# One encoder layer on one core: x handed over in feature order too, and the GLA value projection computed first from x times the norm's vector

## The chip, the cores and the metric

The kernel runs on one core of one Trainium2 chip. The metric is the device time of one execution in microseconds (us). A core has TensorE (matmuls, into eight PSUM banks), VectorE, ScalarE, GpSimd and SyncE; the DMA engines move data between HBM and the core's memory, SBUF. Every engine works through its own instructions in order and waits on semaphores for the others.

## What is computed

A token stream x of 512 tokens by 1024 features goes through one encoder layer: a mixer of neighbourhood attention (NA) and gated linear attention (GLA), then a mixture of 32 experts, then a last norm. The change touches only the first norm and the projections from it, and leaves what is computed as it is. Cut to that:

```python
def rmsnorm(x, g):
    xf = x.astype(jnp.float32)
    y = xf * lax.rsqrt(jnp.mean(xf * xf, axis=-1, keepdims=True) + RMS_EPS)
    return (y * g.astype(jnp.float32)).astype(x.dtype)

def hybrid_mixer(h, w_in, ...):                  # h = rmsnorm(x, norm_mix_g)
    proj = h @ w_in                              # (512 x 1024) @ (1024 x 3104)
    na_q, na_k, na_v, g_q, g_k, g_v, g_r, g_lf, g_lb = jnp.split(proj, cuts, axis=-1)
    ...
```

The parts g_q and g_k (256 columns each) are the GLA queries and keys, g_v (512) its values, g_r (512) its output gate, g_lf and g_lb (16 each) the low-rank inputs of its decay gates. The decay is log_sigmoid(low rank @ w_g2 + b) / 16, summed up within chunks of 64 tokens. All is float32.

The norm's factor of a token, 1/sqrt(mean square + eps), is one number per token, and the norm's vector is one number per feature. So h @ w is (x times the vector) @ w, with each token's result multiplied by its factor.

## The kernel before, in words

The kernel is one function, `mixer_and_moe`, with one instruction stream per engine; the order on each engine is written out by hand, and semaphores tie the streams together. SBUF is one arena in which `at(KiB, ...)` gives a buffer a fixed place, so buffers that lie over each other order the work too.

The start, up to what the change touches:

- **SyncE** (from L347) issues all loads: four token tiles of x (L350, 512 KB each, rows of 4 KB), the constants `small` with the identity matrix (L352, 224 KB), the norm's vector `gmix`, the gate bias, the low-rank weights `w_lr` (L355, 128 KB), `w_g2`, then the weights of the first two groups of 512 columns (L358, 2 MB each): GLA queries and keys, GLA values. Then come the position bias, its mask and late constants. Further groups are loaded into `w_buf` when the group that last used the buffer is done (L369).
- **ScalarE** squares each token tile with a running sum and takes the root (L903, L905); **VectorE** makes mean and reciprocal (L1141, L1143) and scales the tile by the factor into `xs` (L1145).
- **TensorE** transposes each tile in eight pieces (L471); the eight banks then hold x in feature order, eight chunks of 128 features by 512 tokens. VectorE and ScalarE empty them in turn, times the norm's vector, into `hT` (L1150, L899).
- **TensorE** then computes the low-rank product (L509, eight matmuls of 32 columns in four column groups), one unit of queries, the four gate matmuls (L517), three more units of queries and keys, four units of values, four of the output gate. A *unit* is eight matmuls that add up the eight chunks in one bank (`unit`, L487). Units use banks 0 and 1 in turn, the value units banks 2 to 5. ScalarE empties them (`gla_q_evict`, `gv_evict`, L954, L955).
- The gates: ScalarE adds the bias (L926), takes absolute value, exponential and logarithm (L931, L933, L935); VectorE subtracts (L1154), scans by chunk (L1159) and takes differences; ScalarE takes exponentials (L938, L939, L943, L948), VectorE and GpSimd make from them and the queries and keys `q_rel`, `q_exp`, `k_rel` (L1577) and `k_dec` (L1579).
- **GpSimd** builds the 24 bias tables of NA first (L1567), as soon as the mask has landed.

After that TensorE transposes `k_dec` (L532), computes the GLA scores, the NA queries, keys and values with GLA states between them, both attentions, the output projection and the routing. The expert weights (6 MB each expert) are loaded by SyncE upon events of TensorE, the first ones when unit 25 is done (L382); the expert stage begins near 300 us and goes on to 765 us.

Of the kernel before, what the change touches and what calls it, by code (L numbers as in the profile page):

```python
# [60 lines left out]
GV_UNITS = range(5, 9)  # L61
GR_FIRST = range(9, 9 + UNIT_BANKS)
# [25 lines left out]
def mixer_and_moe(nc, x, rpb, w_in, w_g2, b_g, gla_g, g_mix, w_out, g_ffn_T, w_r, b_r, w_gate, w_up, w_down, g_fin,  # L88
                  c_small, c_mask, c_scan, c_tok, out, limit=SLOTS):
    with ExitStack() as ctx:  # L90
# [28 lines left out]
        r_exp = at(78, TT, 512)  # L119
# [4 lines left out]
        xs = at(102, TT, D)  # L124
# [24 lines left out]
        junk = at(179, TT, D)  # L149
# [124 lines left out]
        win_in = [sem(f"win_in{g}") for g in range(7)]  # L274
        og_done, og_added, wog_in, router_ready = sem("og_done"), sem("og_added"), sem("wog_in"), sem("router_ready")
        sumsq_done, ms_done, root_done, rstd_done = sem("sumsq_done"), sem("ms_done"), sem("root_done"), sem("rstd_done")
        xs_done, small_in = sem("xs_done"), sem("small_in")
        xT_done, hT_act, hT_vec = sem("xT_done"), sem("hT_act"), sem("hT_vec")
        unit_done, unit_evicted = sem("unit_done"), sem("unit_evicted")
        gates_done, z_done, abs_done, expa_done = sem("gates_done"), sem("z_done"), sem("abs_done"), sem("expa_done")  # L280
        softp_done, g_done, scan_done, d1_done = sem("softp_done"), sem("g_done"), sem("scan_done"), sem("d1_done")
# [61 lines left out]
        groups = [("lr", None, IN_LR), ("gqk", 0, IN_GQK), ("gv", 1, IN_GV), ("gr", 0, IN_GR),  # L343
# [4 lines left out]
        def _(sp):  # L348
            for t in range(TT):
                sp.dma_start(x1[:, t], x_d[t]).then_inc(x_in_sb[t], 16)  # L350
                if t == 0:
                    sp.dma_start(small[:, 0:448], c_small).then_inc(small_in, 16)  # L352
            sp.dma_start(gmix, g_mix).then_inc(consts_in, 16)
            sp.dma_start(bg, b_g).then_inc(consts_in, 16)
            sp.dma_start(w_lr, win_d[:, :, IN_LR:IN_LR + 2 * RANK]).then_inc(win_in[0], 16)  # L355
            sp.dma_start(gE[:, 0], w_g2).then_inc(consts_in, 16)
            for g in (1, 2):
                sp.dma_start(w_buf[groups[g][1]], win_d[:, :, groups[g][2]:groups[g][2] + 512]).then_inc(win_in[g], 16)  # L358
# [15 lines left out]
            sp.dma_start(w_og[1], wout_d[:, 3 * KC // 4:]).then_inc(wog_in, 16)  # L374
            sp.dma_start(wr_sb, w_r).then_inc(g2_in, 16)
# [90 lines left out]
        def _(pe):  # L466
            pe.wait_ge(small_in, 16)
            for t in range(TT):
                pe.wait_ge(xs_done, t + 1)
                for k in range(KC):  # L470
                    m = pe.transpose(pbank[k][:, t * P:(t + 1) * P], xs[:, t, k * P:(k + 1) * P], ident)  # L471
                    if t == TT - 1:
                        m.then_inc(xT_done, 1)
# [1203 lines left out]
```

## Time and profile before

| | before |
|---|---|
| median of 3 runs | 790.31 us (789.97 to 791.11) |
| profiled execution, its own time | 789.99 us |
| its span | 788.2 us |
| TensorE busy | 735.7 us (93%) |
| VectorE / ScalarE / GpSimd busy | 226.4 / 146.5 / 85.5 us |
| DMA | 234.76 MB, mean 298 GB/s |
| first 20 us: TensorE busy, DMA | 11.1 us, 326 GB/s |

The span is the profiled part of the execution, from its first to its last instruction. Rows of the trace give engines as PE (TensorE matmuls), PEld (its weight loads), DVE (VectorE), ACT (ScalarE), POOL (GpSimd) and SP (SyncE). A float32 matmul of 128x512 leaves two records. PEclk is the granted clock of TensorE as a share of full speed, 2.4 GHz. "L487" is line 487 of the kernel; what stands behind "<-" in square brackets is what ended the engine's idle time.

### The profile page before, as it was taken

What the parts mean: (1) busy time and instruction counts of PE and PEld (TensorE: products, weight loads), DVE (VectorE), ACT (ScalarE), POOL (GpSimd) and SP (SyncE); (2) the same over time, 40 slices, a digit from 0 to 9 for tenths busy, and PEclk for the clock granted to TensorE, in tenths of its full rate; (3) what the DMA queues carried; (4) which work ended last, traced back from release to release, by engine and by line L of the source; (5) the groups of instructions that cost most, each with busy time, mean ns of one, the idle gap of its engine ahead of it and who ended that gap; (6) DMA issues with size and microseconds to landing.
All of it is one profiled execution on the core that took longest, in us unless ns stands there. A gap on an engine that the chain in (4) does not pass through costs nothing.

```text
span 788.2 us, 13656 instructions
## 1 busy us (share of the span) xinstructions
PE 735.7 (93%) x6148; PEld 371.3 (47%) x6148; DVE 226.4 (29%) x455; ACT 146.5 (19%) x319; POOL 85.5 (11%) x81
## 2 busy tenths in 40 slices
PE   5999999999999999999999999999999899988950
PEld 3444454464455466555454455545445355433510
DVE  3008782005566257211111111111111111111126
ACT  5252330024255443000000000000000000000004
POOL 0542340000000121000000000000000000000002
PEclk9999999999999999999999999999999999999995
DMA  9430230401450548999999999999999999999964
GB/s 325 120 106 20 87 108 1 160 4 59 184 243 2 229 197 352 377 422 428 424 422 428 423 426 421 425 425 423 425 426 423 424 421 421 420 420 420 410 264 198
DMA packets 36828, 234.76 MB, mean 298 GB/s; under 512 B 5778, under 2 KB 7186, under 8 KB 18976
## 3 DMA queue, kind: packets, MB, share of 16 engines
q1 hardware_dynamic: 34208, 229.66, 71.5%
q0 software_dynamic: 2560, 4.20, 1.4%
q8 instruction: 50, 0.82, 0.4%
q14 instruction: 10, 0.08, 0.0%
HBM read 227.55 MB, written 10.49 MB: 302 GB/s over the span
## 4 chain that ended last, share of the span: by engine, by line
PE 74%; DMA 19%; SPq 2%; ACT 2%; DVE 1%; issue 1%; DVEq 0%; POOLq 0%
PE bank L487 21%; PE bank L792 18%; DMA arena<-in_w_up 17%; PE bank L815 10%; PE bank L772 8%; PE bank L655 4%; PE bank L699 3%; SPq L419 2%; PE bank L616 1%; PE bank L688 1%; PE bank L673 1%; PE bank L794 1%; PE bank L795 1%; PE bank L804 1%; DMA arena<-in_x 1%; PE bank L718 1%
## 5 line engine op out<-in xcount | busy, mean ns | idle before, releaser
L792 PE MATMUL bank<-arena 128*64 128x512 f32 x928 | 207.0, 597 | 11.4 <-DMA arena<-in_w_up 10.6
L487 PE MATMUL bank<-arena 128*128 128x512 f32 x384 | 167.0, 594 | 0.0
L792 PEld LDWEIGHTS bank<-arena 128*64 128x64 f32 x928 | 68.5, 138 | 144.9 <-issue 135.1
L815 PE MATMUL bank<-arena 128*64 128x512 f32 x512 | 116.9, 598 | 0.5 <-ACT arena L1100 0.5
L487 PEld LDWEIGHTS bank<-arena 128*128 128x128 f32 x384 | 72.3, 190 | 89.8 <-issue 88.6
L772 PEld LDWEIGHTS bank<-arena 128*128 128x128 bf16 x3072 | 96.2, 98 | 23.9 <-issue 23.4
L772 PE MATMUL bank<-arena 128*128 128x64 bf16 x3072 | 100.6, 193 | 0.0
L1095 ACT ACTIVATE arena<-bank,arena 128x256 f32<-128x256 f32 x32 | 15.2, 474 | 359.8 <-PE bank L792 316.4
L1602 POOL DMA_INDIRECT y_tok<-arena x32 | 31.2, 976 | 432.4 <-DVE arena L1473 404.4
L1466 DVE SCALAR_TENSOR_TENSOR arena<-bank,arena 128x256 f32<-128x256 f32 x32 | 15.5, 483 | 214.2 <-ACT arena L1095 214.2
L815 PEld LDWEIGHTS bank<-arena 128*64 128x64 f32 x512 | 33.9, 136 | 57.1 <-issue 54.5
L1137 DVE TENSOR_TENSOR arena<-bank,arena 128x256 f32<-128x256 f32 (+1 forms) x64 | 34.2, 555 | 84.4 <-PE bank L772 67.6
L1137 DVE TENSOR_TENSOR arena<-arena 128x512 f32<-128x512 f32 (+9 forms) x75 | 47.1, 648 | 11.3 <-ACT arena L948 4.0
L1473 DVE COPY arena<-bank 128x512 f32<-128x512 f32 x32 | 22.1, 692 | 94.7 <-PE bank L815 94.7
L655 PE MATMUL bank<-arena 128*128 128x512 f32 x64 | 31.5, 617 | 0.0
L699 PE MATMUL bank<-arena 128*128 128x512 f32 x64 | 28.4, 594 | 0.0
L1595 POOL TENSOR_TENSOR arena<-arena 128x512 bf16<-128x512 f32 x8 | 9.3, 1157 | 174.2 <-ACT arena L1051 174.2
L1100 ACT COPY arena<-bank 128x256 f32<-128x256 f32 x32 | 12.0, 374 | 64.1 <-PE bank L804 64.1
L1567 POOL TENSOR_TENSOR arena<-arena 128x256 f32<-128x256 f32 x24 | 19.4, 845 | 27.8 <-DMA arena<-in_c_mask 27.8
L699 PEld LDWEIGHTS bank<-arena 128*128 128x128 f32 x64 | 11.8, 190 | 13.4 <-issue 13.4
L794 PE MATMUL bank<-arena 128*64 128x256 f32 x96 | 15.6, 381 | 2.1 <-DMA arena<-in_w_up 2.1
L1137 DVE TENSOR_TENSOR arena<-arena,bank 128x512 f32<-128x512 f32 (+1 forms) x17 | 11.1, 654 | 20.3 <-PE bank L699 12.6
(161 smaller groups left out, 466.8 us busy)
## 6 DMA issues: line engine op xcount, KB each, us to landing
arena<-in_w_down SPq DMA_DIRECT2D x31, 2048.0 KB, 30.8
arena<-in_w_gate SPq DMA_DIRECT2D x25, 2048.0 KB, 25.0
arena<-in_w_up SPq DMA_DIRECT2D x24, 2048.0 KB, 23.8
arena<-in_w_up SPq DMA_DIRECT2D x14, 1024.0 KB, 28.2
arena<-in_w_in SPq DMA_DIRECT2D x6, 2048.0 KB, 8.0
arena<-in_w_gate SPq DMA_DIRECT2D x12, 1024.0 KB, 27.2
arena<-y_tok SPq DMA_DIRECT2D x8, 512.0 KB, 5.5
arena<-in_x SPq DMA_DIRECT2D x4, 512.0 KB, 6.3
```

Of the source, the lines that this page charges most:

```text
L419: sp.dma_start(gate_unit(e)[:, ks], wg_d[e][:, ks]).then_inc(landed_in[e % SETS], 16)
L487: m = pe.matmul(pbank[unit_bank(n)][:], lhs(k), rhs(k), start=(k == 0), stop=(k == KC - 1))
L655: mm = pe.matmul(pbank[GLA_BANK[j]][:], yT[:, KC // 2 + k, t * P:(t + 1) * P], w_og[part][:, k % 2, half * 512:(half + 1) * 512], start=(k ...
L699: mm = pe.matmul(pbank[2 * (t % 2) + half][:], yT[:, k, t * P:(t + 1) * P], w_on[:, k, half * 512:(half + 1) * 512], start=(k == 0), stop= ...
L772: mm = pe.matmul(pbank[3][:, k * SLOTS:(k + 1) * SLOTS], h2_part[t][i][:, k], pick[e % RING][:, t], start=(t == 0 and k == 0 and i == 0), ...
L792: mm = pe.matmul(both, xT[:, k], gate_and_up(e, k, cols), start=(k == 0), stop=(k == KC - 1))
L794: pe.matmul(both[:, 0], xT[:, k], gate_unit(e)[:, k, cols], start=(k == 0), stop=False)
L815: mm = pe.matmul(pbank[5 + e % RING][64 * half:64 * half + 64, :], hidT[:, kc % 2, kc // 2], down_unit(e)[:, kc, half * 512:(half + 1) * 512],
L1137: return nc.vector.tensor_tensor(out_, a, b, op)
L1473: nc.vector.tensor_copy(y_sb[e % RING], pbank[5 + e % RING][:]).then_inc(y_evicted, 1)
L1567: nc.gpsimd.tensor_tensor(bias[:, h, v].rearrange("p (j r) -> p j r", r=ROWS), run, mask[:, v].rearrange("p (j r) -> p j r", r=ROWS), ALU. ...
L1602: nc.gpsimd.indirect_dma_start(y_tok, bass.IndirectOffsetOnAxis(ap=tab_u[:, e:e + 1], axis=0), y_sb[e % RING], None, bounds_check=last_row ...
```

## The change

The host hands over x a second time, as `x_T` in feature order (128 x 8 x 512). SyncE loads the norm's vector first, then feature chunks of `x_T` and of the value weights in five pieces (1, 1, 2, 2 and 2 chunks), the low-rank weights among them, and only then x by tokens and the small constants. VectorE multiplies each chunk by the norm's vector into `gx`. TensorE runs the value matmuls chunk by chunk into banks 2 to 5; after chunk 3 it computes the low-rank product and a row of factors, after chunk 4 the gates. The factors per token come as before from x by tokens. As a row across the tokens they are made on TensorE: a matrix of ones times the diagonal matrix of the factors. With the row VectorE scales the low-rank product, and GpSimd makes `hT` from `gx`, ahead of the bias tables. ScalarE applies the factor per token when it empties the value banks. The transposes and `xs` are gone. Queries and keys then follow as four units, then the output gate.

The evictions on ScalarE are placed anew between the exponentials; `r_exp` lies where the mask was, so ScalarE waits for the bias tables before it, and SyncE waits for `rg_done` before it loads the router's weights there.

```diff
@@ sync
+            sp.dma_start(gmix, g_mix).then_inc(xw_in[0], 16)
+            for c, (k0, k1) in enumerate(X_PIECES):
+                sp.dma_start(x_raw[:, k0:k1], x_T[:, k0:k1]).then_inc(xw_in[c], 16)
+                sp.dma_start(w_buf[0][:, k0:k1], win_d[:, k0:k1, IN_GV:IN_GV + 512]).then_inc(xw_in[c], 16)
+                if k1 == 6:
+                    sp.dma_start(w_lr, win_d[:, :, IN_LR:IN_LR + 2 * RANK]).then_inc(lr_in, 16)
             for t in range(TT):
                 sp.dma_start(x1[:, t], x_d[t]).then_inc(x_in_sb[t], 16)
                 if t == 0:
-                    sp.dma_start(small[:, 0:448], c_small).then_inc(small_in, 16)
+                    sp.dma_start(small[:, 0:448], c_small).then_inc(lr_in, 16)
...
+            sp.dma_start(w_buf[1], win_d[:, :, IN_GQK:IN_GQK + 512]).then_inc(win_in[2], 16)
...
+            sp.wait_ge(rg_done, TT)
             sp.dma_start(wr_sb, w_r).then_inc(g2_in, 16)
@@ tensor
-            for t in range(TT):
-                pe.wait_ge(xs_done, t + 1)
-                for k in range(KC):
-                    m = pe.transpose(pbank[k][:, t * P:(t + 1) * P], xs[:, t, k * P:(k + 1) * P], ident)
...
+            def low_rank():
+                pe.wait_ge(lr_in, 32)
+                for k in range(KC):
+                    j = 32 * (k % 4)
+                    pe.wait_ge(gx_done, k + 1)
+                    mm = pe.matmul(pbank[0][j:j + 32], w_lr[:, k], gx[:, k], start=(k < 4), stop=(k >= 4))
+                mm.then_inc(unit_done, 1)
+            def factors_in_row():
+                for t in range(TT):
+                    pe.wait_ge(diag_done, t + 1)
+                    mm = pe.matmul(pbank[7][:, t * P:(t + 1) * P], ones_f, rstd_diag[:, t], start=True, stop=True)
+                mm.then_inc(row_done, 1)
+            def gates():
+                pe.wait_ge(unit_evicted, 1)
+                pe.wait_ge(consts_in, 32)
+                for m in range(4):
+                    if m >= 2:
+                        pe.wait_ge(z_done, m - 1)
+                    pe.matmul(pbank[6 + m % 2][:], gE[:, 0, m * P:(m + 1) * P], lr,
+                              start=True, stop=True).then_inc(gates_done, 1)
...
+                pe.wait_ge(gx_done, k + 1)
+                for t in range(TT):
+                    mm = pe.matmul(pbank[2 + t][:], gx[:, k, t * P:(t + 1) * P], w_buf[0][:, k], start=(k == 0), stop=(k == KC - 1))
...
+                if k == LR_TURN:
+                    low_rank()
+                    factors_in_row()
+                if k == LR_TURN + 1:
+                    gates()
+            count[0] = 1 + len(GV_UNITS)
+            pe.wait_ge(hT_done, KC)
+            pe.wait_ge(win_in[2], 16)
             for m in range(4):
+                weights_stationary(2, m)
+            pe.wait_ge(win_in[3], 16)
+            for t in range(TT):
+                tokens_stationary(3, t)
@@ scalar
+            act.wait_ge(rstd_done, TT)
+            act.wait_ge(unit_evicted, 1)
+            for t in range(TT):
+                act.wait_ge(unit_done, 2 + t)
+                scaled_copy(gv[:, t], pbank[unit_bank(1 + t)][:], rstd[:, t:t + 1]).then_inc(unit_evicted, 1)
+            gla_q_evict(0)
             act.wait_ge(d1_done, 2)
             nc.scalar.activation(gE, gd, ACT.Exp, scale=1.0 / 16).then_inc(e12_done, 1)
             nc.scalar.activation(gz, gd, ACT.Exp, scale=-1.0 / 16).then_inc(e12_done, 1)
+            gla_q_evict(1)
+            gla_q_evict(2)
...
+            gla_q_evict(3)
             act.wait_ge(k_rel_done, 1)
             nc.scalar.activation(gz, gb, ACT.Exp, scale=1.0 / 16).then_inc(e4_done, 1)
...
+            act.wait_ge(bias_done, 3 * NA_HEADS)
@@ vector
+            nc.vector.memset(ones_f, 1.0)
+            for c, (k0, k1) in enumerate(X_PIECES):
+                dve.wait_ge(xw_in[c], 48 if c == 0 else 32)
+                for k in range(k0, k1):
+                    nc.vector.tensor_scalar(gx[:, k], x_raw[:, k], gmix[:, k:k + 1], None, ALU.mult).then_inc(gx_done, 1)
+            dve.wait_ge(lr_in, 32)
             for t in range(TT):
...
-                nc.vector.tensor_scalar(xs[:, t], x1[:, t], rstd[:, t:t + 1], None, ALU.mult).then_inc(xs_done, 1)
+                nc.vector.tensor_scalar(rstd_diag[:, t], ident, rstd[:, t:t + 1], None, ALU.mult).then_inc(diag_done, 1)
+            dve.wait_ge(row_done, 1)
+            nc.vector.tensor_copy(rstd_row, pbank[7][:]).then_inc(row_copied, 1)
+            dve.wait_ge(row_copied, 1)
+            dve.wait_ge(unit_done, 1)
+            tt(lr, pbank[0][:], rstd_row, ALU.mult).then_inc(unit_evicted, 1)
...
+            dve.wait_ge(hT_done, KC)
+            dve.wait_ge(unit_done, 1 + len(GV_UNITS))
@@ gpsimd
+            pool.wait_ge(row_copied, 1)
+            for k in range(KC):
+                nc.gpsimd.tensor_tensor(hT[:, k], gx[:, k], rstd_row, ALU.mult).then_inc(hT_done, 1)
             pool.wait_ge(bias_in, 16 * NA_HEADS + 16)
...
```

## Rows read from the trace of the kernel before

**Rows 1.** Chain of work that ended last, in order of time: start us, us, what

```profile
7.58 1.16 ACT arena L903 x2
...
11.87 0.21 ACT arena L905
...
12.11 0.17 DVE arena L1143
...
14.49 2.94 PE bank L509 x16
17.42 7.06 PE bank L487 x16
24.49 3.43 PE bank L517 x8
27.92 75.55 PE bank L487 x176
```

**Rows 2.** Windows by stage: busy us of each engine, granted clock, DMA share, GB/s

```profile
core 0: us, PE busy (x) PEld busy (x) DVE busy (x) ACT busy (x) POOL busy (x), PEclk, DMA share, GB/s
0.00:20.00 20.00, 11.09 (x54) 6.48 (x55) 7.01 (x16) 10.77 (x19) 0.20 (x4) 1.00 0.93 326
...
500.00:550.00 50.00, 50.00 (x539) 23.66 (x536) 8.10 (x15) 3.02 (x7) 3.88 (x4) 1.00 1.01 424
```

**Rows 3.** Timeline of SyncE's queue, the first expert load

```profile
206.63 0.33 SPq L382 DMA_DIRECT2D arena<-in_w_gate  x1
```

**Rows 4.** Timeline and DMA issues (KB each, median us to landing), second DMA

```profile
1.20 0.41 SPq L352 DMA_DIRECT2D arena<-in_c_small  x1
```

```profile
arena<-in_c_small SPq DMA_DIRECT2D x1, 224.0 KB, 3.8
```

**Rows 5.** Timeline, 7 to 28 us: start us, us, engine, line, operation

```profile
7.36 0.75 DVE L1145 TENSOR_SCALAR arena<-arena 128x1024 f32<-128x1024 f32 x1
8.23 1.57 PEld L471 LDWEIGHTS bank<-arena 128*128 128x128 f32 x8 [8.23 <-issue]
...
13.11 0.86 PEld L471 LDWEIGHTS bank<-arena 128*128 128x128 f32 x8 [0.61 <-DVE arena L1145]
...
17.35 0.30 PEld L487 LDWEIGHTS bank<-arena 128*128 128x128 f32 x2 [0.84 <-DMA arena<-in_w_in]
...
27.10 0.69 ACT L926 ACTIVATE arena<-bank,arena 128x512 f32<-128x512 f32 x1 [0.17 <-PE bank L517]
```

**Rows 6.** Windows of the start, columns as in rows 2

```profile
14.00:16.00 2.00, 1.72 (x12) 0.46 (x12) 2.00 (x4) 2.00 (x4) 0.00 (x0) 1.00 1.05 385
...
0.00:15.60 15.60, 6.69 (x40) 4.95 (x40) 6.29 (x16) 9.70 (x18) 0.20 (x4) 1.00 0.90 309
```

**Rows 7.** TensorE's timeline in the expert stage, starts after an idle gap

```profile
707.07 3.65 PE L792 MATMUL bank<-arena 128*64 128x512 f32 x16 [1.22 <-DMA arena<-in_w_up]
723.28 5.35 PE L792 MATMUL bank<-arena 128*64 128x512 f32 x16 [2.23 <-DMA arena<-in_w_up]
```

**Rows 8.** GpSimd's timeline, 27 to 110 us

```profile
28.25 19.40 POOL L1567 TENSOR_TENSOR arena<-arena 128x256 f32<-128x256 f32 x24 [27.80 <-DMA arena<-in_c_mask]
...
70.60 4.75 POOL L1577 TENSOR_TENSOR arena<-arena 128x2048 f32<-128x2048 f32 x1 [22.95 <-ACT arena L939]
79.59 4.54 POOL L1579 TENSOR_TENSOR arena<-arena 128x2048 f32<-128x2048 f32 x1 [4.24 <-ACT arena L943]
```

**Rows 9.** Timeline of ScalarE and VectorE, the decay gates, 49 to 87 us

```profile
49.05 1.90 ACT L931 ACTIVATE arena<-arena 128x2048 f32<-128x2048 f32 x1
...
55.49 1.91 ACT L935 ACTIVATE arena<-arena 128x2048 f32<-128x2048 f32 x1
```

```profile
57.43 2.29 DVE L1154 SCALAR_TENSOR_TENSOR arena<-arena 128x2048 f32<-128x2048 f32 x1 [41.11 <-ACT arena L935]
59.76 4.57 DVE L1159 TENSOR_TENSOR_SCAN arena<-arena 128x512 f32<-128x512 f32 x4
64.36 2.36 DVE L1137 TENSOR_TENSOR arena<-arena 128x1024 f32<-128x1024 f32 x2
...
81.58 4.69 DVE L1137 TENSOR_TENSOR arena<-arena 128x2048 f32<-128x2048 f32 x1 [4.01 <-ACT arena L948]
```

More of the change, by code:

```diff
@@ L502, in columns_stationary @@
                 unit(lambda k: hT_cols[:, k, b * P:(b + 1) * P], lambda k: w[:, k])
-            pe.wait_ge(win_in[0], 16)
-            for k in range(KC):
-                j = 32 * (k % 4)
-                pe.wait_ge(hT_act if k % 2 else hT_vec, k // 2 + 1)
-                m = pe.matmul(pbank[0][j:j + 32], w_lr[:, k], hT[:, k], start=(k < 4), stop=(k >= 4))
-            m.then_inc(unit_done, 1)
-            count[0] += 1
-            pe.wait_ge(win_in[1], 16)
-            weights_stationary(1, 0)
@@ L514, in _ @@
-            pe.wait_ge(unit_evicted, 1)
-            pe.wait_ge(consts_in, 48)
-            for m in range(4):
-                pe.matmul(pbank[2 + m][:], gE[:, 0, m * P:(m + 1) * P], lr,
-                          start=True, stop=True).then_inc(gates_done, 1)
-            for m in range(1, 4):
-                weights_stationary(1, m)
-            for g in (2, 3):
-                pe.wait_ge(win_in[g], 16)
-                for t in range(TT):
-                    tokens_stationary(g, t)
+            def low_rank():
[5 more added lines that the diff above has]
+                mm.then_inc(unit_done, 1)
@@ new lines, in _ @@
+            for k in range(KC):
+                c = [k0 for k0, k1 in X_PIECES].index(k) if k in [k0 for k0, k1 in X_PIECES] else None
+                if c is not None:
+                    pe.wait_ge(xw_in[c], 48 if c == 0 else 32)
+                pe.wait_ge(gx_done, k + 1)
+                for t in range(TT):
+                    mm = pe.matmul(pbank[2 + t][:], gx[:, k, t * P:(t + 1) * P], w_buf[0][:, k], start=(k == 0), stop=(k == KC - 1))
+                    if k == KC - 1:
+                        mm.then_inc(unit_done, 1)
+                if k == LR_TURN:
[3 more added lines that the diff above has]
+                    gates()
@@ L932, in _ @@
[L932 to L936 removed]
+            nc.scalar.activation(gd, gz, ACT.Abs).then_inc(soft_step, 1)
+            act.wait_ge(soft_step, 1)
+            nc.scalar.activation(gE, gd, ACT.Exp, scale=-1.0).then_inc(soft_step, 1)
+            act.wait_ge(soft_step, 2)
@@ L937, in _ @@
+            nc.scalar.activation(gd, gE, ACT.Ln, bias=1.0).then_inc(soft_step, 1)
+            act.wait_ge(rstd_done, TT)
[4 more added lines that the diff above has]
+            gla_q_evict(0)
             act.wait_ge(d1_done, 2)
```

92 lines of the change are left out of this document (30 added, 62 removed).

## The prediction

> **What bounds the kernel now.** I read the chain of work that ended last first, in order of time [rows 1]. From 17.4 us to 103.5 us it is TensorE alone: projection units without a hole, one unit (eight float32 matmuls of 128x512) every 6.87 us, with four gate matmuls (3.43 us) between. Ahead of that the chain is not TensorE: it is the landing of x, the sums of squares on ScalarE, the scaling on VectorE and the transposes. The windows by stage say the same [rows 2]: in the first 20 us TensorE is busy for 11.1 us, while the DMA engines move 326 GB/s. So the kernel pays about 17 us before its first real unit, and DMA is the resource at work there. Then I looked at what stands behind. The queue of SyncE issues the expert weights on events of TensorE, the first at 206.6 us [rows 3], and in the expert stage the DMA engines run full at 424 GB/s [rows 2]. Both stages are released by TensorE's progress, none by the clock on the wall, so a shift of TensorE's timeline at 103 us passes through to the end one to one. The same execution needs 788.2 us of span and 789.99 us in all.
>
> **What the change does to the start.** It takes away the 32 transposes, the scaling of x per token and the eight evictions of the transposes. In place of these x comes in feature order, VectorE multiplies each feature chunk by the norm's vector, and the GLA value units (32 matmuls, one chunk at a time into four banks) start with the first chunk. The norm's factor is applied at the eviction of these units on ScalarE, and as a row, made by four small matmuls, to the low-rank product (VectorE) and to the eight chunks of hT (GpSimd).
>
> *First matmul.* Three DMAs stand ahead of it (norm vector, 256 KB of x, 256 KB of weights). The second DMA of before, a 224 KB constant, was issued at 1.20 us, took SyncE 0.41 us and landed 3.8 us later [rows 4]; so the third is issued at about 1.65 us and lands at 5.45 us by that row, or 0.6 us sooner, as only 0.53 MB are moved up to it where 0.75 MB (an x tile and the constant) were moved then: 4.9 to 5.5 us. VectorE's chunk is half of a 128x1024 scaling of 0.75 us, 0.4 us [rows 5], and with hand-overs TensorE starts at 5.75 us (5.4 to 6.1), against 17.35 us for the first unit of before. The next chunks cost 3.43 us each on TensorE (four matmuls of 0.86 us, a unit being eight [rows 1]) and 524 KB each of DMA, 1.35 us at 385 GB/s [rows 6], so TensorE sets the pace: four chunks end at 5.75 + 13.7 = 19.5 us.
>
> *TensorE's clock at the start.* The first eight transposes have their weight loads spread over 1.57 us, the last eight over 0.86 us [rows 5]: the first batch ran at about half speed, although the granted clock is given as 1.00 there. Before, this lay in work that waited for VectorE anyhow. Now it falls on value matmuls. What it costs: the one slow stretch that the trace has within dense work [rows 7], 16 matmul records of 5.35 us instead of 3.65 us, so 1.7 us; bounds 0.8 us (the first batch itself) and 3.4 us (two such stretches). I take 1.7: chunks 0 to 3 end at 21.2 us. The Trainium skill, page "TensorE: Matmul & The Clock Gate", Part 1, says that the engine's default state is the throttled one and that activity releases it; the duration of the first batch agrees, the profile's clock column does not. Without this page the sum is the same.
>
> *The low-rank product and the row, put between chunk 3 and chunk 4.* The low-rank product needs all of x (4.2 MB, landed by about 16 us) and the constant of 224 KB. Its eight matmuls took 2.94 us before, in four pairs, since evictions fed them [rows 1]; with all data there they take between two rounds of 0.86 us and 2.94 us. I take 1.7, as four column groups of 32 stand beside each other. The row costs four matmuls of 128x128, 0.2 us each (128 of 512 columns of 0.86), so 0.85 us. On its own TensorE could begin chunk 4 at 21.2 + 1.7 + 0.85 = 23.8 us (22.1 with no slow clock).
>
> *But the row needs the norm's factors, and these need x in token order, whose DMAs now stand behind 4.3 MB.* Up to the last token tile 6.65 MB must be moved. Before, 20 us moved 6.52 MB [rows 2], so 20.4 us by that; at the 385 GB/s of the weights' own stretch [rows 6], from 2.1 us on, 19.4 us. A DMA is seen 1.6 us later than its bytes by this count: the GLA query and key weights end at byte 4.82 MB, which was moved by 15.6 us (309 GB/s up to there [rows 6]), and TensorE waited for them until 17.35 us [rows 5]. So the last tile is there at 21.0 to 22.0 us; I take 21.5. Behind it stand the square and its sum (1.16 us), the root (0.21), and the mean, the reciprocal (0.17 each) [rows 1] and the new 128x128 diagonal (0.2, as the least VectorE step), then 0.2 us of hand-overs: 23.6 us, and one row matmul more, 23.8 us. Both paths give 23.8 us; I take **24.0 us** for chunk 4, bounds 23.0 (early DMA, no slow clock) and 25.5 us (slow clock of 3.4 us).
>
> *The rest of TensorE.* Chunk 4 3.43, gates 3.43, chunks 5 to 7 10.3 us: the value units end at 41.2 us. Then four query/key and four gate-branch units, 8 x 6.87 = 54.9 us: 96.1 us. Before they ended at 103.5 us [rows 1]. **The gain is 7.4 us.** As an account: the start is 11.6 us earlier; given back are 1.7 (low rank inside), 0.85 (row), 1.7 (clock).
>
> **What I costed at nothing, and its cover.** hT on GpSimd: eight 128x512 products from 24.9 us (row 23.8, copied by VectorE in 0.7). A 128x2048 product took 4.75 us there [rows 8], so 1.2 us for 512, 9.5 us in all: done at 34.4 us, needed at 41.2. It could take 1.7 times as long before TensorE waits. Row copy and low-rank eviction on VectorE: two of 0.7 us, done at 25.3 us, needed by the gates at 27.4. The gates now have two banks in turn; ScalarE empties one in 0.69 us [rows 5] while the other's matmul runs 0.86 us, so 0.1 us at most. The eight extra value-path DMAs and the 2.1 MB more lie ahead of the query/key weights: 9.0 MB, landed by 28 us, needed at 41.2. SyncE's new wait (the gated values done) stands ahead of the router's weights; the queue behind it waits later, for the 25th unit, and VectorE finishes these values before the states, which the wait ahead of it (o done) already contains: nothing. Bias tables on GpSimd now follow hT: 34.4 + 19.4 = 53.8 us [rows 8], needed at 69.
>
> *The in-order queue of ScalarE* is the one I checked most, since evictions now stand behind the gate exponentials, and TensorE waits for evictions two units back. Gates evicted 31.6; absolute value, exponential and logarithm with two table loads 8.35 us (from 49.05 to 57.40 us) [rows 9]: 39.9; VectorE's subtraction 2.3, scans 4.6, differences 2.4 [rows 9]: 49.3; two exponentials 3.8 (1.91 each): 53.1 us. The eviction of the second query unit (done 54.9 us) stands behind that and is wanted at 61.8: 6 us of slack. The first gate-branch eviction stands behind the last key eviction (69.3), k_rel on GpSimd (4.75) and an exponential (1.9): 76 to 77.2 us, wanted at 82.4: 5 us of slack.
>
> **The rivals.**
> 1. *The clock falls again at the stop for the factors.* Where the factors are last, TensorE idles up to 1.8 us at 22 us. After a gap of 2.23 us late in the kernel 16 records took 1.7 us longer [rows 7]; after a gap of 1.22 us they took their usual time. Price 1.7 us on what follows: 784.3 us. Against it: both paths are nearly level, so the gap is likely under 1 us. Chance 0.15. The same page of the Trainium skill has idle time bring the throttle back; the gap of 2.23 us agrees, that of 1.22 us shows no such thing.
> 2. *GpSimd and VectorE slow each other down.* The bias tables used to run while VectorE was idle; now they run beside the subtraction, scans and differences. A 128x2048 product on VectorE took 4.69 us where GpSimd's k_dec ran beside it, against 2.29 us for a two-operand instruction of that size alone [rows 8, 9]. Were all 9.3 us of VectorE's doubled, ScalarE's second exponential would end at 62.4 us and TensorE would wait about 1.3 us at 61.8; the bias tables, stretched likewise, still end before 75. Some of this passes on to the later evictions. Price 1 to 3 us: 784.5 us. Chance 0.12.
> 3. *Slower than before: the same ScalarE queue becomes the bound.* TensorE's unit 8 starts when the second query eviction is done. This turns the sign only if VectorE's 9.3 us take 9.3 + 6 + 7.4 = 23 us or more, 2.4 times as long; each us beyond is a us lost. A tripling gives 27.9 us and 795 us. The dearest row shows a factor of 2.05, so the chance is 0.03.
> 4. *The start is not early*: the small pieces land late, say the first at 8 us and the following at 300 GB/s (326 was the mean of the first 20 us). Then factors come at about 28 us and the gain is 3 us: 787 us. Chance 0.06. If x's token tiles alone are that late the result is the same. At 0.02 the shift is eaten up somewhere behind (no change, 790 us).
>
> My own case has the remaining 0.62.
>
> **How the numbers follow.** 789.99 - 7.4 = 782.6 us for an execution like the profiled one, which lay 0.32 us under the median of the three runs; against the median 782.9. I give 782.8 us. Chunk 4 between 23.0 and 25.5 us gives 781.8 to 784.3; half a microsecond for the DMA-bound stage on either side, and the first two rivals, give **781.0 to 786.0 us** for 8 in 10. A difference of about 0.2% (1.6 us) is what a measurement of this kernel can tell from none. Faster by more: 0.93; within: 0.03 (rest of the fourth and the shift that is eaten up); slower: 0.04.
>
> **What the profile of the changed kernel should show.** First value matmul at 5.8 us; its first records 0.86 us apart rather than 0.43 for a few microseconds; a gap of under 2 us ahead of the last row matmul, released by VectorE, and chunk 4 at 24.0 us; GpSimd's eight products of 1.2 us ending by 35 us, none waited for by TensorE; value units ending at 41 us, then no gap; last gate-branch unit at 96 us; first expert load issued near 199 us instead of 206.6; from there the same picture, shifted. Wrong it would be if TensorE waited for hT, if an eviction held a unit between 48 and 96 us, if chunk 4 came after 26 us, or if the end moved by something other than the move of the first expert load.

## The result and the profile after

| | before | changed |
|---|---|---|
| median, 11 runs each | 790.31 us | 793.18 us (791.43 to 795.54) |
| ratio to before, 95% interval | | 1.0037 (1.0024 to 1.0051) |
| profiled execution, its own time / span | 789.99 / 788.2 us | 792.20 / 790.5 us |
| last gate-branch unit done | 103.5 us | 106.2 us |
| first expert load issued | 206.63 us | 209.33 us |

The kernel became 2.9 us slower where 7.4 us of gain were forecast. From the last gate-branch unit on the two traces are the same, shifted: 2.7 us at that unit and at the first expert load [rows 3], 2.3 us at the end of the span. So nearly all of it was decided in the first 106 us. TensorE's timeline of the changed kernel there (start us, us, line, operation; in square brackets the idle time before it and what ended it):

```profile
5.64 15.92 PE L536 MATMUL bank<-arena 128*128 128x512 f32 x32 [5.64 <-DVE arena L1160]
21.49 1.92 PE L510 MATMUL bank<-arena 128*32 128x512 f32 x16
...
25.17 3.60 PE L536 MATMUL bank<-arena 128*128 128x512 f32 x8
28.61 3.85 PE L527 MATMUL bank<-arena 128*128 128x512 f32 x8
32.29 10.46 PE L536 MATMUL bank<-arena 128*128 128x512 f32 x24
42.59 20.76 PE L487 MATMUL bank<-arena 128*128 128x512 f32 x48
68.77 37.39 PE L487 MATMUL bank<-arena 128*128 128x512 f32 x80 [5.42 <-ACT arena L926]
```

The start works as meant: value matmuls (L536) from 5.64 us, queries and keys (L487) from 42.6 us. Then, three units later, TensorE waits 5.42 us for an eviction of ScalarE (L926), and the 80 records after it take 37.4 us where 80 x 0.429 = 34.3 us are due. The windows show why (the column ahead of the last two is the granted clock, 0.50 being 1.2 GHz):

```profile
67.60:69.60 2.00, 0.83 (x1) 0.50 (x2) 0.78 (x1) 1.61 (x3) 0.00 (x0) 0.50 0.00 0
69.60:71.60 2.00, 2.00 (x4) 0.78 (x3) 2.00 (x2) 0.00 (x0) 0.00 (x0) 0.50 0.00 0
71.60:73.60 2.00, 2.00 (x4) 0.91 (x3) 1.79 (x2) 0.18 (x1) 0.00 (x0) 0.50 0.00 0
```

The gap brought the slow clock with it, 3.1 us on top of 5.4. What TensorE waited for stands in the chain of waits, between the gates and the eviction:

```profile
39.66 1.92 ACT arena L947
41.58 0.02 issue
41.60 15.90 DVE arena L1176
57.51 0.02 issue
57.53 4.58 DVE arena L1183 x4
...
64.53 1.91 ACT arena L955
66.44 1.80 ACT arena L956
68.24 0.49 ACT arena L926
68.73 0.04 issue
68.77 37.40 PE bank L487 x80
```

One instruction of VectorE, the subtraction of the gates (L1176), is there for 15.9 us. The same instruction took 2.29 us before [rows 9]. Beside it GpSimd runs, and ends before it does:

```profile
26.15 9.86 POOL L1586 TENSOR_TENSOR arena<-arena 128x512 f32<-128x512 f32 x8 [25.70 <-DVE arena L1170]
35.95 19.40 POOL L1593 TENSOR_TENSOR arena<-arena 128x256 f32<-128x256 f32 x24
```

GpSimd's 24 bias tables (L1593) follow the hT products without a hole and end at 55.35 us; they took 19.40 us before too [rows 8]. VectorE's instruction ends at 57.50 us, 2.15 us later: as if it had begun when GpSimd was through.

### The profile page after: what moved, and what is told of

It reads as the page before. It is cut to its first block, busy times and chain, and to the rows that moved or that the text cites. A ratio compares the mean times of both kernels' runs of the same rounds, so it can differ in the third digit from the quotient of the medians.

```text
span 790.5 us, 13633 instructions
## 1 busy us (share of the span) xinstructions
PE 734.3 (93%) x6124; PEld 369.2 (47%) x6124; DVE 235.8 (30%) x462; ACT 143.6 (18%) x314; POOL 95.3 (12%) x89
## 4 chain that ended last, share of the span: by engine, by line
PE 69%; DMA 18%; DVE 4%; ACT 4%; SPq 4%; issue 1%; DVEq 0%; POOLq 0%
PE bank L819 18%; DMA arena<-in_w_up 17%; PE bank L487 15%; PE bank L842 10%; PE bank L799 8%; PE bank L682 4%; PE bank L726 3%; DVE arena L1176 2%; SPq L428 1%; PE bank L643 1%; PE bank L715 1%; SPq L429 1%; PE bank L700 1%; DMA arena<-in_x 1%; PE bank L821 1%; PE bank L822 1%
## 5 line engine op out<-in xcount | busy, mean ns | idle before, releaser
L487 PE MATMUL bank<-arena 128*128 128x512 f32 x320 | 142.3, 604 | 5.4 <-ACT arena L926 5.4
L799 PEld LDWEIGHTS bank<-arena 128*128 128x128 bf16 x3072 | 96.2, 98 | 23.6 <-issue 23.1
L487 PEld LDWEIGHTS bank<-arena 128*128 128x128 f32 x320 | 61.4, 194 | 81.4 <-issue 75.1
L1489 DVE SCALAR_TENSOR_TENSOR arena<-bank,arena 128x256 f32<-128x256 f32 x32 | 15.5, 484 | 213.4 <-ACT arena L1112 213.3
L1154 DVE TENSOR_TENSOR arena<-bank,arena 128x512 f32<-128x512 f32 (+1 forms) x65 | 34.9, 557 | 84.5 <-PE bank L799 67.6
L1154 DVE TENSOR_TENSOR arena<-arena 128x512 f32<-128x512 f32 (+9 forms) x75 | 42.8, 591 | 22.3 <-ACT arena L967 12.6
L536 PE MATMUL bank<-arena 128*128 128x512 f32 x64 | 30.0, 627 | 5.6 <-DVE arena L1160 5.6
L682 PE MATMUL bank<-arena 128*128 128x512 f32 x64 | 31.5, 617 | 0.0
L726 PE MATMUL bank<-arena 128*128 128x512 f32 x64 | 28.4, 594 | 0.0
L536 PEld LDWEIGHTS bank<-arena 128*128 128x128 f32 x64 | 12.8, 204 | 21.1 <-issue 15.5
L1176 DVE SCALAR_TENSOR_TENSOR arena<-arena 128x2048 f32<-128x2048 f32 x1 | 15.9, 15893 | 14.8 <-ACT arena L947 14.8
L1593 POOL TENSOR_TENSOR arena<-arena 128x256 f32<-128x256 f32 x24 | 19.4, 852 | 0.0
## 6 DMA issues: line engine op xcount, KB each, us to landing
arena<-in_w_up SPq DMA_DIRECT2D x24, 2048.0 KB, 23.6
```

Of the source, the lines that this page charges most:

```text
L487: m = pe.matmul(pbank[unit_bank(n)][:], lhs(k), rhs(k), start=(k == 0), stop=(k == KC - 1))
L536: mm = pe.matmul(pbank[2 + t][:], gx[:, k, t * P:(t + 1) * P], w_buf[0][:, k], start=(k == 0), stop=(k == KC - 1))
L682: mm = pe.matmul(pbank[GLA_BANK[j]][:], yT[:, KC // 2 + k, t * P:(t + 1) * P], w_og[part][:, k % 2, half * 512:(half + 1) * 512], start=(k ...
L726: mm = pe.matmul(pbank[2 * (t % 2) + half][:], yT[:, k, t * P:(t + 1) * P], w_on[:, k, half * 512:(half + 1) * 512], start=(k == 0), stop= ...
L799: mm = pe.matmul(pbank[3][:, k * SLOTS:(k + 1) * SLOTS], h2_part[t][i][:, k], pick[e % RING][:, t], start=(t == 0 and k == 0 and i == 0), ...
L1154: return nc.vector.tensor_tensor(out_, a, b, op)
```

## The experiments

Theories: **L**, VectorE's two-operand instruction waits as long as GpSimd's series goes on; **S**, the two share bandwidth; **O**, the subtraction is slow for another reason; **M**, something else in the change holds the kernel too. Experiments 1, 2, 8 and 16 were executed four times and 12 six times; the others ran once, so their times are single values and the argument rests on their traces.

**1. Take the overlap away.** GpSimd waits for VectorE's differences ahead of the tables.

```diff
             pool.wait_ge(bias_in, 16 * NA_HEADS + 16)
+            pool.wait_ge(d1_done, 2)
```

> The changed kernel with one wait more: GpSimd starts the 24 bias tables only when VectorE has made the decay differences. Theory L (VectorE's two-operand instructions cannot start their work while GpSimd runs instruction after instruction, and the subtraction's 15.9 us are 13.6 us of waiting): the subtraction takes 2.3 us, the second query unit is evicted in time, and TensorE has no gap between 43 and 77 us. The bias tables then end at about 70 us, which makes q_rel late: I expect up to 1 us of gap at each of two later units, the last gate-branch unit at 98 to 99 us instead of 106.2, and 785 us (784 to 786.5). Rival O (the subtraction is slow for a reason of its own, such as its operands or the gates' late end): it stays at 15.9 us and the time at 793 us or more. Rival M (something else in the change also holds the kernel, so that removing the stall does not move the end one to one): the gap goes but the time falls by less than 5 us.

```profile
41.96 2.29 DVE L1176 SCALAR_TENSOR_TENSOR arena<-arena 128x2048 f32<-128x2048 f32 x1 [14.81 <-ACT arena L947]
```

```profile
42.95 55.10 PE L487 MATMUL bank<-arena 128*128 128x512 f32 x128
```

The subtraction is back at 2.29 us (first fence), TensorE runs its eight units without a gap (second), even the two small ones that I expected are missing, and the median is 784.66 us, ratio to before 0.9931 (0.9915 to 0.9948). Against the changed kernel that is 8.5 us, the gap of 5.4 and the slow clock of 3.1. L and S stand, O and M fall.

**2. Keep the overlap, but with pauses.** Each table waits for the one before.

```diff
             for v in range(3):
...
+                if h or v:
+                    pool.wait_ge(bias_done, 3 * h + v)
                 nc.gpsimd.tensor_tensor(bias[:, h, v]...
```

> The changed kernel, GpSimd's bias tables at their old place, but each waits for the end of the one before. Theory L with the condition that the series runs without a pause: VectorE gets in at the first pause, so the subtraction takes at most 0.85 + 2.3 = 3.2 us, the four scans and two differences at most 0.85 us more each, TensorE has no gap, last gate-branch unit at 97.7 us, 784 us. Rival S (the two engines share bandwidth and each runs slower, pauses or not): the subtraction still takes over 10 us and the time stays near 793 us. Rival L1 (the lock goes to whoever asks first and is given back after each instruction anyway): the same as without pauses, 15.9 us, as this kernel then differs in nothing.

```profile
41.76 2.93 DVE L1176 SCALAR_TENSOR_TENSOR arena<-arena 128x2048 f32<-128x2048 f32 x1 [14.81 <-ACT arena L947]
44.72 6.93 DVE L1183 TENSOR_TENSOR_SCAN arena<-arena 128x512 f32<-128x512 f32 x4
```

```profile
36.09 32.78 POOL L1595 TENSOR_TENSOR arena<-arena 128x256 f32<-128x256 f32 x24
```

VectorE is let in at once, and the engines take turns: the scans take 6.93 instead of 4.57 us, the tables 32.8 instead of 19.4 us. The median is 785.74 us, 0.9935 (0.9918 to 0.9952). S falls: the same two series overlap, and shared bandwidth would slow the subtraction with or without a pause of GpSimd.

**3. Split the subtraction** into four pieces of 128x512.

```diff
-            nc.vector.scalar_tensor_tensor(gz, gz, 0.0, gd, ALU.min, ALU.subtract).then_inc(g_done, 1)
-            dve.wait_ge(g_done, 1)
+            for m in range(4):
+                nc.vector.scalar_tensor_tensor(gz[:, m], gz[:, m], 0.0, gd[:, m], ALU.min, ALU.subtract).then_inc(g_done, 1)
+            dve.wait_ge(g_done, 4)
```

> The changed kernel, the subtraction on VectorE in four pieces of 128x512 instead of one of 128x2048. Theory L: the first piece holds the whole wait (about 14 us), the other three take 0.6 us each; time as the changed kernel, 792 to 795 us. Rival S (sharing): the four pieces take about 4 us each. Rival O (the size or form of the one instruction is the trouble): the pieces take 0.6 us each and the stall is gone.

All instructions of this line, as min/median/max in ns:

```profile
L1177 DVE SCALAR_TENSOR_TENSOR arena<-arena x4: 677/678/14310, 41.6 to 57.1; 128x512 f32<-128x512 f32 x4
```

One piece of 14.31 us, three of 0.68 us; 792.9 us. The time is waiting, not work: sharing would have slowed all four.

**4. The same overlap in the kernel before**, with nothing of the change.

```diff
             pool.wait_ge(bias_in, 16 * NA_HEADS + 16)
+            pool.wait_ge(expa_done, 1)
```

> The kernel before with one wait more: GpSimd starts the bias tables when the exponential of the gates is done, about 54.2 us, so that they run to 73.6 us, across VectorE's subtraction. Nothing of the change is in it. Theory L: the subtraction, asked for at 57.4 us, is recorded at about 18 us instead of 2.3, ending near 75.8 us; q_exp and with it the first gate-branch eviction come some 10 us later, TensorE waits about 6 us near 90 us and runs slowly for some microseconds after, and the time rises by 6 to 10 us, to 796 to 800 us. Rival S: the subtraction takes 5 us at most and the time rises by under 3 us. Rival O (the stall belongs to the new layout of buffers): the subtraction stays at 2.3 us.

```profile
57.28 2.31 DVE L1154 SCALAR_TENSOR_TENSOR arena<-arena 128x2048 f32<-128x2048 f32 x1 [41.11 <-ACT arena L935]
```

```profile
54.17 31.14 POOL L1568 TENSOR_TENSOR arena<-arena 128x256 f32<-128x256 f32 x24 [53.72 <-ACT arena L933]
```

The time came as forecast (799.8 us), the way it came did not. VectorE was let in after four tables, with no pause in the series, and it was GpSimd that became late: tables of 31.1 us, so k_rel and everything behind it late, and TensorE waited 8.11 us for the first gate-branch eviction. So L as I had it fell: a series without pauses does not always hold VectorE. What differs between this run and the changed kernel?

**5 to 7. The phase.** In the changed kernel VectorE asked at the very start of a GpSimd instruction (41.60 us for both). Theory P: it is this that makes it lose; rival Q: it is what GpSimd has done before. A fill of 64 or 256 columns ahead of the subtraction, or one of 128 columns on GpSimd ahead of the tables, moves that.

```diff
# 5 and 6, vector
             dve.wait_ge(soft_step, 3)
+            nc.vector.memset(at(208, 64), 0.0)        # 6: 256 columns
# 7, gpsimd
+            nc.gpsimd.memset(at(208, 128), 0.0)
             pool.wait_ge(bias_in, 16 * NA_HEADS + 16)
```

> The changed kernel with a small fill (64 columns, about 0.1 us) on VectorE ahead of the subtraction, into a place that nobody uses. In the changed kernel and in its split form VectorE's request came in the same nanosecond or next to it as the start of a GpSimd instruction (41.606 beside 41.605 us), and it waited for the end of the whole series; in the three runs in which it came 0.07, 0.5 and 0.7 us into one, it went in before the next. Theory P (it is the phase: a request that meets the start of a GpSimd instruction loses to the whole series): with the request 0.1 us later VectorE goes in at the next boundary, the subtraction takes about 3 us and the time is 784 to 786 us. Rival Q (it is the history: GpSimd's series has run without any pause since 26 us, over the hT products, and such a series is not interrupted): the subtraction still takes about 15.8 us and the time is 792 to 795 us.

> As the short shift, with 256 columns: the request comes about 0.3 us into a GpSimd instruction. Theory P: the subtraction takes 2.3 to 2.9 us, 784 to 786 us. Rival Q: about 15.6 us, 792 to 795 us.

> The changed kernel with a small fill (128 columns) on GpSimd between the hT products and the bias tables. It moves GpSimd's phase by 0.1 to 0.3 us and puts an instruction that reads no SBUF into the series. Theory P: VectorE goes in at the next boundary, 784 to 786 us. Theory Q with the break of the series by a fill: the same. Theory Q without it (only a wait breaks a series): the subtraction stays at 15 to 16 us, 792 to 795 us. With the two shifts of VectorE this tells what kind of thing decides.

The subtraction took 15.82, 15.66 and 16.02 us, the times were 792.5, 792.0 and 794.7 us. P fell three times over: VectorE asked 0.08, 0.29 and 0.66 us into a GpSimd instruction and was held each time. Nor does the fill, which reads no SBUF, break the series.

**9, 10, 11. How much went before.** One pause ahead of the tables; one pause after the fourth hT product; and in the kernel before, the tables started so that VectorE asks late in the series. Theory N: the number of instructions since GpSimd last waited decides; R: only pauses all through the series help; S0: it matters how the series began.

```diff
# 9
+            pool.wait_ge(hT_done, KC)
             pool.wait_ge(bias_in, 16 * NA_HEADS + 16)
# 10
             for k in range(KC):
+                if k == 4:
+                    pool.wait_ge(hT_done, 4)
# 11, kernel before
             pool.wait_ge(bias_in, 16 * NA_HEADS + 16)
+            pool.wait_ge(unit_evicted, 4)
```

> The changed kernel with one pause in GpSimd's series: it waits for its own last hT product ahead of the first bias table. The phase fell as a cause (three shifted kernels were held as long). What is left: in the runs in which VectorE was let in, it asked 7 or 3 instructions after GpSimd's last wait; in those in which it was held, 15 or 16 after. Theory N (VectorE is held by a series only if more than about 8 instructions have gone by since GpSimd last waited): now it asks 7 after the pause, goes in at the next boundary, subtraction about 3 us, 784 to 786 us. Rival R (the series must be broken at every instruction, or while VectorE waits): held until the series ends, subtraction 15.9 us, 792 to 795 us.

> The same single pause four instructions earlier, between the fourth and the fifth hT product, so that VectorE asks 11 or 12 instructions after it. Theory N with a number near 8: held, 15.9 us, 792 to 795 us. If any pause between GpSimd's first instruction and VectorE's request is enough, whatever its distance (theory S0: what matters is how the series began, on the heels of a VectorE instruction at 26 us): subtraction 3 us, 784 to 786 us.

> The kernel before, GpSimd's bias tables released by the eviction of the third query/key unit at 42.3 us, so that they run to 61.7 us and VectorE's subtraction asks at 57.4 us, 18 instructions after GpSimd's last wait, with 5 left. Theory N: it is held to the end of the series, recorded at 6 to 6.7 us instead of 2.3, and the rest of VectorE's gate work runs undisturbed; the whole shifts by 4 us, under the slack of this kernel: 790 to 792 us. Theory S0: it goes in at the next boundary (2.3 to 3.1 us), and its successors take turns with the five tables.

One pause was enough at either place: subtraction 2.33 and 2.34 us, 784.9 and 786.0 us. R fell. And the kernel before can be held too:

```profile
57.80 6.60 DVE L1154 SCALAR_TENSOR_TENSOR arena<-arena 128x2048 f32<-128x2048 f32 x1 [41.11 <-ACT arena L935]
```

6.60 us: 4.45 us until the last table ends, five more after the one that was running, and its own 2.15. S0 fell with that, and the effect needs nothing of the change. The time was 795.5 us, not 790 to 792: I had taken this kernel's slack for 4 us, and TensorE waited 2.05 us for the first gate-branch eviction, and the 32 records after it took 2 us too long (15.70 us).

**13 to 15. Number or time.** After the pause of experiment 10 the last four products in four pieces each (many instructions, little time); a pause after the second product (in the middle); no pause, but the eight products as two instructions (few, and long). Theory T: the time since GpSimd last waited decides, against N.

```diff
# 13, with the pause of 10
-                nc.gpsimd.tensor_tensor(hT[:, k], gx[:, k], rstd_row, ALU.mult).then_inc(hT_done, 1)
+                for c in range(4 if k >= 4 else 1):
+                    cs = slice(c * P, (c + 1) * P) if k >= 4 else slice(0, T)
+                    m = nc.gpsimd.tensor_tensor(hT[:, k, cs], gx[:, k, cs], rstd_row[:, cs], ALU.mult)
+                m.then_inc(hT_done, 1)
# 15, no pause; all waits on hT_done for 2
+            for k in (0, 4):
+                nc.gpsimd.tensor_tensor(hT[:, k:k + 4], gx[:, k:k + 4], rstd_row.unsqueeze(1).broadcast_to((P, 4, T)),
+                                        ALU.mult).then_inc(hT_done, 1)
```

> The changed kernel with one pause after the fourth hT product (as the tenth experiment, in which VectorE was let in 11 instructions and 10.4 us after it), and the last four products in four pieces each, so that VectorE asks some 22 instructions but only about 11 us after the pause. Theory N (the number of instructions since GpSimd last waited decides, with a limit between 11 and 16): held, the subtraction takes over 12 us, 791 to 796 us. Theory T (the time decides, limit between 10.4 and 15 us): let in, 2.3 to 3.1 us, 784 to 787 us.

> The changed kernel with one pause after the second hT product, so that VectorE asks in the 13th or 14th instruction and about 12.9 us after it. Both theories have their limit in this gap; the run halves it. Let in: about 785 us; held: 792 us or more.

> The changed kernel without any pause, the eight hT products as two instructions of 128x2048. VectorE asks in the 10th instruction but about 15.4 us after GpSimd's last wait. Theory N: let in, subtraction 2.3 to 3.1 us, 784 to 786 us. Theory T: held, 15.9 us, 792 to 796 us.

The windows from GpSimd's last wait to VectorE's request count its instructions (busy us and, in brackets, number; GpSimd is the fifth pair). Experiment 13, then 15, each with its subtraction:

```profile
31.78:42.24 10.46, 10.46 (x26) 4.73 (x25) 0.00 (x0) 9.77 (x9) 10.43 (x21) 1.00 0.19 52
...
42.24 17.73 DVE L1176 SCALAR_TENSOR_TENSOR arena<-arena 128x2048 f32<-128x2048 f32 x1 [14.81 <-ACT arena L947]
```

```profile
26.50:41.98 15.48, 15.48 (x37) 6.66 (x36) 0.67 (x1) 11.07 (x10) 15.45 (x11) 1.00 0.51 125
...
41.98 2.96 DVE L1176 SCALAR_TENSOR_TENSOR arena<-arena 128x2048 f32<-128x2048 f32 x1 [14.81 <-ACT arena L947]
```

21 instructions in 10.5 us hold VectorE (795.1 us), 11 in 15.5 us do not (784.6 us). So the **number** decides, not the time. VectorE's first request that met a series, in the runs with at most one pause in it, by the number since GpSimd last waited and the time since then:

| run | number | us | VectorE's instruction |
|---|---|---|---|
| 4 | 4 | 3.1 | let in, 2.31 us |
| 8 (the product for q_rel) | 6 | 4.2 | let in, 2.88 us |
| 9, 16 | 7 | 5.6 | let in, 2.33 and 2.32 us |
| 1 (the product for q_rel) | 8 | 6.2 | let in, 2.49 us |
| 10 | 11 | 10.4 | let in, 2.34 us |
| 15 | 11 | 15.5 | let in, 2.96 us |
| 14 | 15 | 14.2 | held, 14.78 us |
| changed kernel, 3, 5, 6, 7 | 15 or 16 | 15.5 to 15.7 | held, 15.7 to 16.1 us |
| 11 | 19 | 15.0 | held, 6.60 us |
| 13 | 21 | 10.5 | held, 17.73 us |

For these first requests the limit lies between 11 and 15 instructions. It is not simply a count since GpSimd's last wait. In experiments 4, 9, 10, 15 and 16 VectorE idles and asks a second time within the same series, when GpSimd has issued 13, 19, 23, 23 and 19 instructions without a wait, and is let in each time. Experiment 15, VectorE's second request and GpSimd's series:

```profile
59.75 6.16 DVE L1154 TENSOR_TENSOR arena<-arena 128x2048 f32<-128x2048 f32 x3 [4.33 <-ACT arena L926]
35.49 31.13 POOL L1594 TENSOR_TENSOR arena<-arena 128x256 f32<-128x256 f32 x24
```

VectorE's three instructions end at 65.9 us, and the series goes on to 66.6. What these second requests have in common is that VectorE had kept GpSimd standing only 2 to 5 instructions earlier. So all runs agree with a count since GpSimd last stood still, be it for a wait or for a turn of VectorE. No run tests this by itself, and what in the engines makes it, none shows.

**8, 12, 16. A version that beats both.** The tables late or with pauses, the low-rank product one chunk later, and two matmuls of ones ahead of the first chunk, against the slow clock.

```diff
-LR_TURN = 3
+LR_TURN = 4
...
+            pe.wait_ge(diag_done, 2)
+            for _ in range(2):
+                pe.matmul(pbank[7][:], ones_f, rstd_row, start=True, stop=True)
...
```

> The changed kernel with the bias tables after the decay differences (as in the first experiment), the low-rank product and the row one chunk later (after chunk 4), and two matmuls of ones ahead of the first chunk, while TensorE waits for x. From the changed kernel's trace the first ten records at 0.85 instead of 0.43 us cost 2.1 us, in the first experiment's twice as long. If activity ahead of the first chunk ends the slow clock sooner, the value units end 2 to 3 us earlier, at 40 us instead of 42.9, and the time falls from 784.7 to 782 us. If the clock rises no sooner, or if the factors' row is late anyhow, the value units end at 42 us or later and the time stays at 784 to 785 us.

> The changed kernel with pauses between the bias tables at their old place (second experiment), the low-rank product one chunk later and two matmuls of ones ahead of the first chunk (eighth experiment). The eighth had 1.5 us of gap at 83 us, as its bias tables ended late and k_rel with them; with the tables at their old place k_rel follows the last key eviction at 68.5 us, and no gap is left: last gate-branch unit at 95.3 us instead of 97.0, 782.3 us. If the second experiment's 785.7 us show a cost of the pauses beyond the trace, it stays at 784 us.

> The twelfth experiment with one wait of GpSimd ahead of its first bias table instead of one ahead of each. VectorE asks at about 42.7 us, 8 or 9 instructions after the wait, and is let in. GpSimd saves the 0.1 us between tables. Last gate-branch unit at 95.3 us and 782 to 783.5 us, as the twelfth. If it is held: 790 us or more.

TensorE in experiment 12:

```profile
1.60 3.78 PE L532 MATMUL bank<-arena 128*128 128x512 f32 x4 [1.60 <-DVE arena L1161]
5.70 17.95 PE L540 MATMUL bank<-arena 128*128 128x512 f32 x40 [0.32 <-DVE arena L1165]
...
40.42 55.10 PE L487 MATMUL bank<-arena 128*128 128x512 f32 x128
```

The matmuls of ones take the slow stretch: forty value records in 18.0 us (in experiment 8 in 17.4), where 17.2 is full speed and the changed kernel needed 15.9 us for 32. Value units end at 40.4 us. Experiment 8: 783.97 us; 12: **783.01 us**, 0.9901 (0.9882 to 0.9921); 16: 783.29 us, 0.9911 (0.9895 to 0.9928). Experiment 8 kept 1.5 us of gap at 83 us, the others none. Between 12 and 16 there is no difference that these runs show.

That a shift of TensorE at 100 us passes through holds for all of them (start of the transposes of k_dec, first expert load, the same execution's time):

| | transposes | first expert load | time |
|---|---|---|---|
| before | 103.29 | 206.63 | 789.99 |
| changed | 106.00 | 209.33 | 792.20 |
| 1 | 97.88 | 201.22 | 784.48 |
| 9 | 97.63 | 200.97 | 784.85 |
| 12 | 95.36 | 198.69 | 782.95 |
| 4 | 113.39 | 216.72 | 799.76 |

The first two columns move together exactly, the time within 0.9 us of them.

## Why the prediction was wrong, step by step

**The reading of what bounds the kernel held.** TensorE's timeline at 103 us sets the end (table above).

**The start held, with three terms off.**
- First value matmul: 5.75 us, measured 5.64.
- Slow clock at the start: forecast 1.7 us. The first five records stand 0.85 us apart until 9.2 us and the rest 0.43, 2.1 us too much (3.2 in experiment 1, whose 32 records took 17.0 us).
- Low rank and row: chunks 0 to 3 end at 21.5 us (21.2 forecast), the low-rank product takes 1.9.
- The last factor: forecast 23.6 us from the landing of the last token tile, measured 24.8. The tile itself came about as forecast, by 21.7 us (21.5). (The lag of a DMA behind its bytes was 17.35 - 15.6 = 1.75 us by its rows, not 1.6; nothing turned on it.) The first tile was squared at 17.2 us only, and then ScalarE did four tiles one behind another, each 1.46 us, with a table load of 1.28 after the first. The term that failed is that I timed the chain from the last transfer, when a chain on one engine from the first transfer was longer.
- Gates 3.7 instead of 3.43 us, as the third waited for its bank. Value units end at 42.6 us, forecast 41.2.

So the start alone would have given 5.5 us of gain, 1.9 less than forecast: experiment 9, which leaves the whole change in place and adds one wait, ran 784.9 us, and experiment 1, 784.66.

**hT on GpSimd held**: done at 36.0 us (34.4 forecast), waited for by nobody.

**The step that failed is the price of GpSimd and VectorE running side by side**, and by it the cover of ScalarE's queue. I named the right place (the second rival: tables beside the subtraction; the third: the eviction of the second query unit behind it), and took the price from the right row, in the wrong way. The 128x2048 product beside k_dec took 4.69 us, and I read a rate, a factor of 2.05. Read by its ends, that row says something else: VectorE's started at 81.58 us and ended at 86.27; GpSimd's ended at 79.59 + 4.54 = 84.13 [rows 8, 9]; from there it is 2.14 us, VectorE's own time. It had waited for the end of the other and then run at full speed. A factor grows with the instruction's own time, a wait with the other engine's. With a wait as the price the bound would have been all the tables still queued: by my own times 53.8 - 39.9 = 13.9 us instead of the 2.3 of a doubling. VectorE's chain of 9.3 us would then take 23.2, just where the third rival turns the sign. I had given that rival 0.03. The Trainium skill says it outright, on its page "SBUF — State Buffer", section "SBUF: two separate sides": the port pair that VectorE and GpSimd share is an exclusive lock held for a whole instruction, and the loser fully blocks. The row of before agrees, and so does experiment 2, where the subtraction took 2.93 us, the rest of one table and its own time. In the changed kernel VectorE was kept out for longer than the instruction that was running: for the 16 tables behind it as well.

How the 13.6 us became 2.9: VectorE's chain ended at 64.5 us; the eviction had 8.2 us of slack by the chain's own end (I had put 6, which is the slack of the unit, done later than the chain); 5.4 us of gap remained. This is the sign of being wrong that I had named, an eviction that holds a unit between 48 and 96 us. The gap brought 3.1 us of slow clock, the very mechanism of the first rival, at another place. 97.7 us (the value units' end and eight units) plus 8.5 is the measured 106.2, against 103.5 before.

**Had the engines taken turns**, the gain would have been about 5 us: experiments 9 and 10 (784.9 and 786.0), in which the tables overlap VectorE's work as in the changed kernel but let it in, show that. That they lie near the second rival's 784.5 us is luck. Its mechanism, a wait of TensorE of 1.3 us near 62 us, did not come: the eight units run without a gap in both, and VectorE's chain took 12.8 us in experiment 9 (41.71 to 54.55), 3.5 more than alone and not twice as long. What made them slower than my forecast is the start, whose value units end at 42.7 and 43.0 us instead of 41.2. What no row of before could show is that a series of fifteen instructions keeps VectorE out until its last. Before, the tables ran while VectorE had nothing to do.

## What to carry to other kernels

When two engines share something, read the overlap by its ends: who started, who ended, and how long after. If the loser ends its own time after the winner, the price is a wait, and its bound is all that the winner has queued, not a factor. In this kernel GpSimd's long series was cheap only while VectorE had no two-operand work; one wait in it, on its own last result and at most 11 instructions ahead of VectorE's request, gave VectorE its turn (8.3 us here for one line). And TensorE's idle gap of 5.4 us cost 3.1 us more than itself.

## What the runs showed of the hardware that I had not expected

- A series of GpSimd's products and sums of two SBUF operands let VectorE's first two-operand request in at the next boundary where 11 or fewer had been issued since GpSimd last waited, and kept it out until the series ended where 15 or more had. A fill in the series broke nothing; a wait for GpSimd's own last result, 0.08 us long, did. Once VectorE had had a turn it got in again after 13 to 23 instructions without a wait, so a turn seems to act as a wait does.
- Once they take turns, each of VectorE's scans beside a table costs 0.6 us more (four take 6.93 instead of 4.57 us), and each of GpSimd's tables waits for the end of VectorE's instruction (24 tables 31 to 33 us instead of 19.4 where the subtraction, scans and differences all ran beside them).
- After being kept out VectorE ended 2.14 to 2.15 us after GpSimd did, in the row of before and in every run where the undivided subtraction was held.
- The slow clock at the start is not in the granted-clock column (1.00 from the first microsecond): it is seen only by records 0.85 us apart instead of 0.43. After the gap at 63 us the column does show 0.50. The gap of 1.53 us in experiment 8 cost 0.1 us beyond itself, that of 2.05 us in experiment 11 cost 2 us more.
